# The context rows of eight modulation chunks weighed by GpSimd instead of VectorE

## The reference, cut to what matters

```python
s_lat = silu(c)[:, None, :]
s_ctx = silu(c_ctx)[None, None, :]
for i in range(DEPTH):
    mod_l = split(s_lat @ ada_w[i] + ada_b[i], 6, axis=-1)
    mod_c = split(s_ctx @ ada_w[i] + ada_b[i], 6, axis=-1)
    h_lat = modulate(x_lat, mod_l[0], mod_l[1])
    h_ctx = modulate(x_ctx, mod_c[0], mod_c[1])
    y_ctx, y_lat = retention_mixer(h_ctx, h_lat, ...)   # 4 heads in layer 0
    ...
```

## Time and profile before

| What | Value |
|---|---|
| Runs, median (lowest to highest) | 2050.21 us (2049.97 to 2050.42) |
| Profiled execution, own time | 2049.45 us |
| Its span, first to last instruction | 2047.7 us |
| Granted TensorE clock | 0.996 of full |
| Busy: PE, DVE, ACT, POOL | 1990.2, 1287.7, 850.0, 68.4 us |
| Heads, 42.68 to 400 us: PE busy | 346.60 of 357.32 us |
| The same: DVE busy, POOL busy | 278.44, 18.55 us |

### The profile page before, as it was taken

How to read it: one execution, slowest core, us unless ns; L and a number is a source line. 1 busy time by engine, 2 the same in 40 slices (tenths; PEclk the granted TensorE clock), 3 DMA queues, 4 the chain that set the end, 5 groups by cost and what they waited for, 6 DMA issues and landing times.

```text
span 2047.7 us, 26988 instructions
## 1 busy us (share of the span) xinstructions
PE 1990.2 (97%) x11062; PEld 1689.6 (83%) x11062; DVE 1287.7 (63%) x1584; ACT 850.0 (42%) x993; POOL 68.4 (3%) x121
## 2 busy tenths in 40 slices
PE   5999999999999999999989999999999999999998
PEld 3778787778888888877779998899899978989997
DVE  3878869556555344586766555766855567677555
ACT  5322323223322122355665443654544356545442
POOL 0000000000111000000000000000000000000000
PEclk9999999999999999999999999999999999999999
DMA  9543434334454343233137654555655554546552
GB/s 337 185 153 124 144 126 142 123 109 128 139 167 139 118 138 139 90 116 103 42 103 213 185 177 151 187 170 170 216 188 189 180 169 158 196 162 210 191 187 73
DMA packets 250733, 319.28 MB, mean 156 GB/s; under 512 B 10097, under 2 KB 166034, under 8 KB 250098
## 3 DMA queue, kind: packets, MB, share of 16 engines
q1 hardware_dynamic: 234880, 262.24, 39.9%
q0 software_dynamic: 14416, 53.14, 7.8%
q10 hardware_dynamic: 1314, 2.18, 0.3%
HBM read 316.47 MB, written 1.05 MB: 155 GB/s over the span
## 4 chain that ended last, share of the span: by engine, by line
PE 76%; DVE 12%; DVEq 5%; ACT 2%; issue 1%; SPq 1%; ACTq 1%; DMA 1%
PE ps L2270 12%; PE ps L2271 12%; PE ps L2265 6%; PE ps L2811 6%; PE ps L2817 5%; PE ps L2821 5%; PE ps L2818 5%; PE ps L2284 4%; PE ps L2280 4%; PE ps L2281 4%; PE ps L2213 3%; DVE raw L1357 2%; PE ps L2731 2%; PE ps L2728 2%; PE ps L2727 2%; DVE w_lo L1240 2%
## 5 line engine op out<-in xcount | busy, mean ns | idle before, releaser
L1240 DVE TENSOR_TENSOR w_lo<-raw,w_hi 128x2048 fp32r<-128x2048 f32 (+1 forms) x244 | 553.1, 2272 | 314.2 <-ACT w_hi L600 313.5
L600 ACT ACTIVATE w_hi<-raw 128x2048 fp32r<-128x2048 f32 (+1 forms) x244 | 461.9, 1897 | 264.7 <-PE ps L2265 161.3
L2270 PE MATMUL ps<-w_hi,big_hi 128*128 128x512 f32 x760 | 298.6, 393 | 1.1 <-DVE big_lo L1711 0.8
L2271 PE MATMUL ps<-w_hi,big_lo 128*128 128x512 f32 x760 | 296.1, 390 | 0.0
L2280 PE MATMUL ps<-hT_hi,w_hi 128*128 128x512 f32 (+1 forms) x512 | 192.2, 380 | 3.1 <-ACT arena L711 2.0
L2281 PE MATMUL ps<-hT_lo,w_hi 128*128 128x512 f32 (+1 forms) x512 | 190.1, 376 | 0.0
L2817 PE MATMUL ps<-h_hi,w_hi 128*128 128x256 f32 x768 | 189.6, 285 | 0.0
L2818 PE MATMUL ps<-h_lo,w_hi 128*128 128x256 f32 x768 | 188.3, 283 | 0.0
L2270 PE MATMUL ps<-w_hi,hT_hi 128*128 128x512 f32 x416 | 167.9, 403 | 6.4 <-DVE hT_lo L1245 6.4
L2270 PEld LDWEIGHTS ps<-w_hi,big_hi 128*128 128x128 f32 x760 | 142.8, 188 | 30.6 <-DVE big_lo L1711 1.1
L2271 PEld LDWEIGHTS ps<-w_hi,big_lo 128*128 128x128 f32 x760 | 142.8, 188 | 29.1 <-issue 0.5
(11 more groups left out here) (304 smaller groups left out, 3047.7 us busy)
## 6 DMA issues: line engine op xcount, KB each, us to landing
raw<-ffn_w_in SPq DMA_DIRECT2D x88, 512.0 KB, 5.1
raw<-w_in SPq DMA_DIRECT2D x80, 512.0 KB, 4.6
raw<-w_up SPq DMA_DIRECT2D x64, 512.0 KB, 4.8
raw<-w_down SPq DMA_DIRECT2D x64, 512.0 KB, 4.5
raw<-ret_w_in SPq DMA_DIRECT2D x48, 512.0 KB, 5.6
front<-ada_w POOLq DMA_DIRECT2D x24, 1024.0 KB, 5.5
raw<-ffn_w_out SPq DMA_DIRECT2D x40, 512.0 KB, 4.3
raw<-ada_w POOLq DMA_DIRECT2D x64, 256.0 KB, 4.1
```

The costliest lines, as they stand in the source:

```text
L600: act.activation(SPLIT_HI[PAIR_OF[u]][:, 0:m], raw[:, RAW_OF[u], 0:m], ACT.Copy).then_inc(sem["hi_ready"], 1)
L1240: op(SPLIT_LO[PAIR_OF[u]][:, 0:m], raw[:, RAW_OF[u], 0:m], SPLIT_HI[PAIR_OF[u]][:, 0:m].bitcast(F32), ALU.subtract).then_inc(sem["lo_ready ...
L2270: pe.matmul(out, x[0][:, t * P:(t + 1) * P], w, start=start, stop=False)
L2271: pe.matmul(out, x[1][:, t * P:(t + 1) * P], w, start=False, stop=False)
```

## The change

A constant `BY_POOL = 8` is added. For chunks 0 to 7 VectorE weighs only row 0, the latent row; GpSimd weighs row 1, the context row, in a new function `weigh_ctx`. GpSimd has no fused multiply-add here: it multiplies into a temporary `POOL_TMP` and adds, with a drain behind each. A new semaphore `ctx_used` counts its pieces; `extra` on TensorE waits for it, and so does `on_hi(2)` on ScalarE, which writes over the temporary. GpSimd's list of loads is rebuilt round `weigh_ctx`, and it waits for `at_full` before it writes an accumulator set again. Chunks 8 to 19 are as before.

```diff
+BY_POOL = 8
...
+        POOL_TMP = FRONT_IN[2][:, 0, :]
...
+            def weigh_ctx(c, j):
+
+                ks, rows = piece(c, j)
+                pool.wait_ge(ada_in[j], 16 * (c + 1))
+                acc = acc_of(c)[0][:, 1, :]
+                for x, k in enumerate(ks):
+                    i = pool.tensor_scalar(acc if k == 0 else POOL_TMP, rows[:, x, :], SZ[:, k, 1:2], None, ALU.mult)
+                    pool.drain()
+                    if k:
+                        i = pool.tensor_tensor(acc, acc, POOL_TMP, ALU.add)
+                        pool.drain()
+                i.then_inc(sem["ctx_used"], 1)
+
             pool.wait_ge(sem["front_used"], 4)
-            for c in range(EARLY):
+            for j in range(2):
+                load(0, j)
+            for c in range(1, EARLY):
+                if c <= BY_POOL and c > 2:
+                    pool.wait_ge(sem["at_full"], 4 + c - 2)
                 for j in range(2):
-                    if c:
-                        pool.wait_ge(sem["ada_used"], 2 * c - 1 + j)
+                    if c <= BY_POOL:
+                        weigh_ctx(c - 1, j)
+                    pool.wait_ge(sem["ada_used"], 2 * c - 1 + j)
                     load(c, j)
...
             def on_hi(h):
                 act.wait_ge(sem["ot_mul"], h + 1)
+                if h == 2:
+                    act.wait_ge(sem["ctx_used"], 2 * BY_POOL)
...
-                        for m in rows_of(c):
+                        for m in (0,) if c < BY_POOL else rows_of(c):
...
                 pe.wait_ge(sem["ada_used"], done)
+                if c < BY_POOL:
+                    pe.wait_ge(sem["ctx_used"], 2 * (c + 1))
```

More of the change, by code:

```diff
@@ L229, in build @@
                  "rstd_ready", "on_hi", "on_lo", "ident_in", "sz_set", "cols_full", "cols_read",
-                 "xt_full", "xt_read", "xm_ready", "h_part", "front_used", "xc_in", "ada_used", "row_ready", "at_full",
+                 "xt_full", "xt_read", "xm_ready", "h_part", "front_used", "xc_in", "ada_used", "ctx_used", "row_ready", "at_full",
                  "mod_ready", "qk_read", "g_read", "qkt_full", "qkt_read", "sc_full", "sc_read", "v_read",
```

## The result

The changed kernel takes 2126.85 us, the median of 4 runs (2125.09 to 2128.41), against 2050.27 us (4 runs) before. The ratio is 1.0374, with a 95% interval of 1.0361 to 1.0387: 76.6 us slower. 2062 was forecast, with a range up to 2079. The sign was right, the size was six times too small.

A forecast was written before the change was run, and what follows sets the result against it. PE was taken to bound the heads: three places of 5.3 us less 3.15 (+12.7) and -0.8 for the values' wait made about +12 us on 2049.45, 2061.4, so 2062 as the runs' median; range 2047 to 2079.

The forecast's parts named there:

- PE bounds the heads, and VectorE's relief is worth at most 4.8 us: Retention heads: VectorE's 39 us saved count only where PE waits for chunks 1, 4, 7 and two heads' values, 4.8 us.
- A multiply 0.8, an add 1.2, a drain 0.1, piece 1 8.8 us: GpSimd's assumed costs in us per 128 x 512 operation; four multiplies, four adds and eight drains make piece 1 8.8 us.
- A chunk is 16 us, GpSimd keeps pace, so it weighs the late piece from 86.9: Three chunks take GpSimd 49 us in a head of 89, so chunk 1's piece 1 starts at 86.9.
- the late piece: Piece 1 of chunk 1, and likewise of 4 and 7: eight GpSimd operations forecast at 8.8 us just before PE asks.
- the 99.8 of the forecast: Forecast end of GpSimd's piece 1 of chunk 1: 95.7 undisturbed plus 4.1 us held up by VectorE.
- the 5.3: PE's forecast wait in us at each of chunks 1, 4 and 7, against 3.15 for all three before.
- The rival: GpSimd operations at the double make piece 1 17.6 us, three places 15 us each, +42; half that excess +29, 2079; chance 0.14.
- GpSimd is released by VectorE's first piece (85.8), since the load stands ahead of the eight operations: Chunk 1: GpSimd's in-order list first issues chunk 2's piece 0 load, which waits until VectorE ends its piece at 85.8.
- Places: PE waits for GpSimd's adds at chunks 1, 4 and 7, some 5 us each, and not at chunks 0, 3 or 6.
- Disturbance: Before PE's call, VectorE's four multiply-adds and half a low part hold GpSimd up by 4.1 us, between nothing and 5.3.

The follow-up runs named there:

- x1b_half_alone: The kernel before, but VectorE weighs only the latent rows of chunks 0 to 7 and nobody weighs their context rows: 2046.34 us, ratio 0.9978.
- x2b_sem: The changed kernel with each drain of GpSimd replaced by a wait for its own semaphore: 2091.44 us, ratio 1.0201.
- x4b_first_piece: The changed kernel, but GpSimd weighs only piece 0 of each context row and VectorE adds the other four slabs: 2079.23 us, ratio 1.0144.
- y1_spare: As x1b_half_alone, plus 15 GpSimd operations a chunk on spare data, with semaphore waits between them, that nobody waits for: 2067.69 us, ratio 1.0086.
- y2: The changed kernel with BY_POOL = 2, so GpSimd weighs the context rows of chunks 0 and 1 alone: 2079.22 us, ratio 1.0139.
- y3: x4b_first_piece with semaphores for drains, the multiply as a spread TENSOR_TENSOR, and the weighing ahead of the load that waits: 2077.63 us, ratio 1.0137.
- y4: x2b_sem with GpSimd's multiply written as a tensor_tensor with a spread column: 2099.12 us, ratio 1.0242.

## Why the prediction was wrong, step by step

- *PE bounds the heads, and VectorE's relief is worth at most 4.8 us.* Right: x1b_half_alone gave 4.5, and VectorE's saving of 39 us was 39.9.
- *A multiply 0.8, an add 1.2, a drain 0.1, piece 1 8.8 us.* This term was mis-sized. The add was right (1.26), the multiply is 1.56, nearly twice. I had drawn it from the memset's slope, which a copy does follow. The drain is 0.17, but 3.3 us and more behind a load; that cost was in no term. Undisturbed, piece 1 is 4 x 1.56 + 4 x 1.26 + 6 x 0.16 + 3.3 = 15.5 us; from 107.25 to 122.82 it took 15.6.
- *A chunk is 16 us, GpSimd keeps pace, so it weighs the late piece from 86.9.* This is the step that failed, and the larger part of the miss. GpSimd's own work is 36.7 us a chunk against the 29.8 of PE's head. In head 0 the three pieces before took 16.8, 17.6 and 17.5 us, in place of 7.5 to 8.8, and the late piece began at 107.25, 20.4 us later than forecast. It ended at 122.8, 23.0 later than the 99.8 of the forecast; PE asked at 101.8, 7.1 later; that turns the 5.3 into 21.2. With the measured 15.6 in the forecast's own path, from 86.9 on, a place would have cost 8 us and the whole some 21, so the late piece alone explains little.
- *The rival.* "GpSimd is the pace" was the case. Its point of decision, 1.5 us for an operation and its drain, was passed: piece 1 has 15.6/8 = 1.95. But I had priced it, too, by the late piece alone (+42 at the double). With the pace lost, GpSimd comes to chunk 4's first piece only at 202.61, when chunk 3's second is done; its accumulator was free since 190.0. PE asks at 213.3, in the middle of the first piece, and stands until the second is done, to 237.0.
- *GpSimd is released by VectorE's first piece (85.8), since the load stands ahead of the eight operations.* The order is so, but in head 0 this wait was over long before: GpSimd itself came to the load at 87.5 for the piece before, and at 106.4 for this one. VectorE, hindered, ended the piece at 90.4, not 85.8. The path is there once GpSimd is faster: in x2b_sem this wait is the last at chunks 4 and 7, and in x4b_first_piece it makes GpSimd late.
- *Places.* Right: chunks 1, 4 and 7. I said that chunks 0, 3 and 6 would not be waited for; 4.2, 0.39 and 0.37 us were.
- *Disturbance.* The mechanism was right, and larger than taken. GpSimd's operations are 4.3 us a chunk longer, VectorE's loss eats 35 of its 39 us, and by itself the hindering costs about 22 us (y1_spare), more than my whole forecast. I had counted it in the window before PE's call and nearly nowhere else, while VectorE's whole chain leads up to that call.
- *The clock.* Left out: PE is busy 8.9 us more, at a granted clock of 0.86 to 0.90 in the heads with holes.

The parts don't add up to 76.6, and shouldn't: without drains 35 us go, without PE's direct wait 25, and the hindering alone makes 22. Of x2b_sem's remaining 41 us the estimate for chunk 4 gives 4.6 of 11.5 to the bare length of GpSimd's operations behind the in-order wait and 6.9 to the hindering of both engines; no run took the two apart.

## What to carry to other kernels

Before moving work to GpSimd, measure the very form of the operation there: its multiply of a tile took three times what its memset did. Count its loads with it, since they share one list, and a drain behind a load held it up for 3.3 us and more; a semaphore wait in its place didn't. Add up the engine's whole list over a head and compare it with the head, before pricing the one late piece. And look at what VectorE does at that time: here its path was mostly operations with two inputs from SBUF, GpSimd's help was taken back in blocking, and a relief that could win 4.5 us didn't pay for it in any of the six forms tried (the change, x2b, x4b, y2, y3, y4).

## What the runs showed of the hardware that was not expected

- GpSimd on 128 x 512 float32: memset 0.52 us, copy 0.61, TENSOR_TENSOR with a spread column 1.04, add 1.28, TENSOR_SCALAR 1.49 with a constant and 1.56 with a value per partition.
- A drain on GpSimd behind a load it has issued: 3.3 us of pause for a load of 1 MB, 5.0 for one of 128 x 640; a semaphore wait behind the next load 0.1. What it waits for, no run showed.
- A shorter form of an operation on GpSimd (1.04 for 1.56) made the kernel slower, 1.0242 against 1.0201, and VectorE's multiply-adds longer. That its second read is the cause was not tested.
